# Second mixer of a three-layer kernel: gate steps shifted, compressed keys in another PSUM bank, a diagonal made earlier, scores with turned sign

## The reference, cut to what matters

```
z = rms_norm(x, ln1_g) @ w_in                       # mq mk mv mo mi mf aq akc avc aks avs akw avw ag
# mLSTM, 4 heads of 128: gates from mi, mf (log-sigmoid, running sum, running maximum), then per head
h = num / max(|den|, exp(-m));  h = rms_norm(h, mlstm_norm_g) * sigmoid(mo)
# attention, 8 heads of 64 in 2 groups, three branches, each a softmax with a distance penalty:
Kc, Vc = gelu(blocks(akc) @ ck_w1) @ ck_w2, gelu(blocks(avc) @ cv_w1) @ cv_w2      # 31 compressed keys
s = q . k / 8 - slope * distance;  p = softmax(s, masked);  o = p @ v
a = gate0 * o_compressed + gate1 * o_selected + gate2 * o_window
x = x + concat(h, a) @ w_out
```

## Time and profile before

| what | value |
|---|---|
| median of 3 runs | 1643.48 us (1639.96 to 1644.78) |
| the profiled execution's own time | 1649.33 us |
| its span, first to last instruction | 1647.6 us |
| mean granted TensorE clock | 0.985 |
| PE busy (matmul) | 1598.9 us, 97% |
| DVE busy | 1023.2 us, 62% |
| ACT busy | 706.1 us, 43% |
| POOL busy | 172.3 us, 10% |

### The profile page before, as it was taken

How to read it: one execution, slowest core, us unless ns; L and a number is a source line. 1 busy time by engine, 2 the same in 40 slices (tenths; PEclk the granted TensorE clock), 3 DMA queues, 4 the chain that set the end, 5 groups by cost and what they waited for, 6 DMA issues and landing times.

```text
span 1647.6 us, 21391 instructions
## 1 busy us (share of the span) xinstructions
PE 1598.9 (97%) x8046; PEld 1295.3 (79%) x8046; DVE 1023.2 (62%) x1926; ACT 706.1 (43%) x1391; POOL 172.3 (10%) x148
## 2 busy tenths in 40 slices
PE   7999999999998999999999999999998999999997
PEld 7888888888875788888888887766665888888887
DVE  6876666645667586766653376666666555554367
ACT  6544444333456545444432333344344344433242
POOL 0021111000012202111110000000010001110000
PEclk9999999999998999999999999999999999999998
DMA  6133333332110213333322424221110233333331
GB/s 221 52 109 96 97 101 96 103 115 97 61 58 26 75 55 100 98 94 94 101 96 98 140 98 116 53 51 39 39 39 20 90 96 96 97 97 100 96 109 64
DMA packets 91151, 143.69 MB, mean 87 GB/s; under 512 B 8740, under 2 KB 30756, under 8 KB 90920
## 3 DMA queue, kind: packets, MB, share of 16 engines
q1 hardware_dynamic: 88560, 136.58, 27.0%
q10 hardware_dynamic: 2488, 5.75, 1.1%
HBM read 140.19 MB, written 2.10 MB: 86 GB/s over the span
## 4 chain that ended last, share of the span: by engine, by line
PE 91%; DVE 4%; issue 2%; ACT 2%; DMA 1%; SPq 0%; POOL 0%; DVEq 0%; POOLq 0%; ACTq 0%
PE ps L433 23%; PE ps L435 23%; PE ps L434 23%; PE ps L1915 2%; PE ps L1917 2%; PE ps L1916 2%; PE ps L474 2%; PE ps L476 1%; PE ps L475 1%; PE ps L1597 1%; PE ps L1620 1%; PE ps L1640 1%; PE ps L1293 1%; PE ps L1322 1%; PE ps L1242 1%
## 5 line engine op out<-in xcount | busy, mean ns | idle before, releaser
L418 DVE TENSOR_TENSOR wl<-raw,wh 128x512 fp32r<-128x512 f32 (+2 forms) x425 | 307.3, 727 | 406.9 <-ACT wh L409 406.6
L409 ACT ACTIVATE wh<-raw 128x512 fp32r<-128x512 f32 (+2 forms) x425 | 264.5, 627 | 554.2 <-PE ps L435 549.6
L433 PE MATMUL ps<-Hh,wh 128*128 128x512 f32 x1148 | 453.1, 395 | 3.1 <-DVE Hl L1486 1.9
L434 PE MATMUL ps<-Hl,wh 128*128 128x512 f32 x1148 | 448.6, 391 | 0.0
L435 PE MATMUL ps<-Hh,wl 128*128 128x512 f32 x1148 | 448.5, 391 | 0.0
L433 PEld LDWEIGHTS ps<-Hh,wh 128*128 128x128 f32 x1148 | 216.3, 188 | 51.7 <-issue 2.7
L434 PEld LDWEIGHTS ps<-Hl,wh 128*128 128x128 f32 x1148 | 216.5, 189 | 45.4 <-issue 0.7
L435 PEld LDWEIGHTS ps<-Hh,wl 128*128 128x128 f32 x1148 | 216.4, 189 | 45.5
L433 PE MATMUL ps<-AH,wh 128*128 128x512 f32 x416 | 161.8, 389 | 0.0
L434 PE MATMUL ps<-AL,wh 128*128 128x512 f32 x416 | 161.8, 389 | 0.0
L435 PE MATMUL ps<-AH,wl 128*128 128x512 f32 x416 | 161.8, 389 | 0.0
(11 more groups left out here) (335 smaller groups left out, 2191.5 us busy)
## 6 DMA issues: line engine op xcount, KB each, us to landing
raw<-in_w_in SPq DMA_DIRECT2D x216, 256.0 KB, 2.7
raw<-in_w_out SPq DMA_DIRECT2D x104, 256.0 KB, 2.6
raw<-in_w_up SPq DMA_DIRECT2D x64, 256.0 KB, 2.7
raw<-in_w_down SPq DMA_DIRECT2D x32, 256.0 KB, 2.6
raw<-in_w_q SPq DMA_DIRECT2D x16, 256.0 KB, 2.6
raw<-in_w_o SPq DMA_DIRECT2D x16, 256.0 KB, 2.6
raw<-in_w_pg SPq DMA_DIRECT2D x16, 256.0 KB, 2.6
X<-in_xT SPq DMA_DIRECT2D x8, 256.0 KB, 4.6
```

The costliest lines, as they stand in the source:

```text
L409: e.activation(split_in[n][0][:, 0:width], raws[n % NRAW][:, 0:width], ACT.Copy, scale=1.0 if gain is None else gain).then_inc(s_hi, 1)
L418: e.tensor_tensor(wl[:, 0:width], raw, wh[:, 0:width].bitcast(F32), ALU.subtract).then_inc(s_lo, 1)
L433: e.matmul(b, wh[:, o:o + w], xh, start=k == 0, stop=False, skip_group_check=joined)
L434: e.matmul(b, wh[:, o:o + w], xl, start=False, stop=False, skip_group_check=joined)
```

## The change

It touches the second mixer only.

1. `gates` 1, 2, 3 and 4 stand later: after `z1` 4, `z1` 6, `z2` 0 and `z2` 2. Abs, Exp and Ln become an entry of their own on ACT, `logs`, after `z1` 3.
2. The compression uses bank `turned[7]` (`CMP_BANK`) in place of the gates' bank. `cmp` 1 no longer waits for `s_gcol` 2, but for `s_zev` 10, the end of `take 1`.
3. In beat 0, (`m`, 0, 0) stands ahead of `unit` 0, and the first two column tiles wait for `s_zev` 11 and 12 in place of 13.
4. L1892 and L1896 of step 7 (the diagonal) become an entry of their own, `lstm_diag`, ahead of `sums` in the same beat, and so ahead of that beat's split, `mtake` and `turn` on DVE; for head 3 it stands ahead of `w0` 4.
5. Queries are scaled by -0.125, the distance tables have the other sign, the maxima become minima, and the exponentials take scale -1. L1710 falls away, and with it two of DVE's own waits in a unit.

```diff
         for k in range(1, 8):
             MIX += [("z1", k)]
-            MIX += [("gates", k // 2 - (k == 2))] if k in (2, 4, 6) else [("blocks", 2 * (k // 2) + i) for i in range(2)]
-            MIX += [("gates", 1)] * (k == 3)
+            MIX += [("gates", k // 2 - 1)] if k in (2, 4, 6) else [("blocks", 2 * (k // 2) + i) for i in range(2)]
+            MIX += [("logs",)] * (k == 3)
         MIX += [("take", 1)]
         for k in range(8):
-            MIX += [("z2", k)] + [("cmp", k)] * (1 <= k <= 6) + [("gates", 4)] * (k == 0)
+            MIX += [("z2", k)] + [("cmp", k)] * (1 <= k <= 6) + [("gates", 3 + k // 2)] * (k in (0, 2))
...
         for b in range(NU + 3):
-            MIX += [("unit", b)] + [("m", b, 0)] * (b < 32) + [("sums", b)]
+            MIX += [("m", 0, 0), ("unit", 0)] if b == 0 else [("unit", b)] + [("m", b, 0)] * (b < 32)
+            MIX += [("lstm_diag", LSTM[b - 8][0])] * (b >= 8 and LSTM[b - 8][1] == 7)
+            MIX += [("sums", b)]
...
-        MIX += [("w0", 3), ("fill", 6), ("w0", 4), ("lstm", *LSTM[31]), ("w0", 5), ("w0", 6), ("fill", 7), ("w0", 7)]
+        MIX += [("w0", 3), ("fill", 6), ("lstm_diag", 3), ("w0", 4), ("lstm", *LSTM[31]), ("w0", 5), ("w0", 6), ("fill", 7), ("w0", 7)]
...
                     for g in range(2):
-                        e.tensor_tensor_reduce(Sb[u % 4][:, g, 0:L], turned[4 + g][:, 0:L], bias[:, 4 * g + r, S - L:S],
-                                               1.0, -3e38, ALU.add, ALU.max,
-                                               unit_sc(u, 0)[:, g:g + 1]).then_inc(s_vst, 1)
-                    step += 2
-                    e.wait_ge(s_vst, step)
-                    e.tensor_scalar(unit_sc(u, 1), unit_sc(u, 0), -1.0, None, ALU.mult).then_inc(s_sm, 1)
+                        m = e.tensor_tensor_reduce(Sb[u % 4][:, g, 0:L], turned[4 + g][:, 0:L],
+                                                   bias[:, 4 * g + r, S - L:S], 1.0, 3e38, ALU.add, ALU.min,
+                                                   unit_sc(u, 1)[:, g:g + 1])
+                    m.then_inc(s_sm, 1)
...
             elif s == 7:
-                c0, c1 = lane_col(h, 0), lane_col(h, 1)
-                e.wait_ge(s_mpow, h + 1)
-                e.scalar_tensor_tensor(c1, c1, 0.5, c0, ALU.mult, ALU.mult).then_inc(s_mdx, 1)
-                e.wait_ge(s_mdx, h + 1)
-                if h > 0:
-                    e.wait_ge(s_mbr, h)
-                e.tensor_tensor(DG[:, :, :], ident[:, :].unsqueeze(1).to_broadcast([P, 4, P]),
-                                c1.unsqueeze(2).to_broadcast([P, 4, P]), ALU.mult).then_inc(s_mdg, 1)
                 e.wait_ge(s_mbr, h + 1)
...
+        def dve_lstm_diag(e, h):
+            c0, c1 = lane_col(h, 0), lane_col(h, 1)
+            e.wait_ge(s_mpow, h + 1)
+            e.scalar_tensor_tensor(c1, c1, 0.5, c0, ALU.mult, ALU.mult).then_inc(s_mdx, 1)
+            e.wait_ge(s_mdx, h + 1)
+            if h > 0:
+                e.wait_ge(s_mbr, h)
+            e.tensor_tensor(DG[:, :, :], ident[:, :].unsqueeze(1).to_broadcast([P, 4, P]),
+                            c1.unsqueeze(2).to_broadcast([P, 4, P]), ALU.mult).then_inc(s_mdg, 1)
...
                     if t < 4 and t % 2 == 0 and half == 0:
-                        e.wait_ge(s_zev, 13)
+                        e.wait_ge(s_zev, 11 + t // 2)
...
-        GATE_BANK = 3
+        GATE_BANK, CMP_BANK = 3, 7
         def pe_compress(e, k):
-            hb = turned[GATE_BANK]
+            hb = turned[CMP_BANK]
             if k == 1:
                 e.wait_ge(s_w1, 32)
-                e.wait_ge(s_gcol, 2)
+                e.wait_ge(s_zev, 10)
...
+        def act_logs(e):
+            e.wait_ge(s_gst, 2)
+            e.activation(T[7][0:4, :], T[5][0:4, :], ACT.Abs).then_inc(s_gac, 1)
+            e.wait_ge(s_gac, 1)
+            e.activation(T[7][0:4, :], T[7][0:4, :], ACT.Exp, scale=-1.0).then_inc(s_gac, 1)
+            e.wait_ge(s_gac, 2)
+            e.activation(T[7][0:4, :], T[7][0:4, :], ACT.Ln, bias=1.0).then_inc(s_gac, 1)
...
-                    e.scalar_tensor_tensor(big[:, at_, :], b, 0.125, RB[:, :], ALU.mult, ALU.mult).then_inc(s_zev, 1)
+                    e.scalar_tensor_tensor(big[:, at_, :], b, -0.125, RB[:, :], ALU.mult, ALU.mult).then_inc(s_zev, 1)
```

More of the change, by code:

```diff
@@ L1650, in act_unit @@
                     pv = Sb[u % 4][:, :, 0:124]
-                    e.activation(pv, pv, ACT.Exp).then_inc(s_ex, 1)
+                    e.activation(pv, pv, ACT.Exp, scale=-1.0).then_inc(s_ex, 1)
                 else:
@@ L1655, in act_unit @@
                         sx = Sb[u % 4][:, g, 0:L]
-                        m = e.activation(sx, sx, ACT.Exp, bias=unit_sc(u, 1)[:, g:g + 1],
+                        m = e.activation(sx, sx, ACT.Exp, scale=-1.0, bias=unit_sc(u, 1)[:, g:g + 1],
                                          accum_out=unit_sc(u, 2)[:, g:g + 1])
@@ L1695, in dve_unit @@
                         e.wait_ge(s_vst, step + 1)
-                        e.tensor_reduce(cmp_sc(g, 0), pv, AX, ALU.max).then_inc(s_vst, 1)
+                        e.tensor_reduce(cmp_sc(g, 0), pv, AX, ALU.min).then_inc(s_vst, 1)
                         e.wait_ge(s_vst, step + 2)
@@ L2023, in act_gates @@
         def act_gates(e, k):
-            R = lambda i: T[i][0:4, :]
             if k == 0:
@@ L2028, in act_gates @@
                              ACT.Sigmoid).then_inc(s_gsg, 1)
[L2029 to L2034, removed]
             elif k == 4:
@@ L2091, in act_second @@
                     e.activation(hid[:, :, 0:62],
-                                 turned[GATE_BANK][:, 128:256].rearrange("p (i n) -> p i n", i=2)[:, :, 0:62],
+                                 turned[CMP_BANK][:, 128:256].rearrange("p (i n) -> p i n", i=2)[:, :, 0:62],
                                  ACT.Gelu_apprx_tanh).then_inc(s_gelu, 1)
@@ L2100, in act_second @@
                     act_gates(e, i[0])
+                elif what == "logs":
+                    act_logs(e)
                 elif what == "unit":
@@ L2176, in dve_second @@
                     dve_unit_turn(e, i[0] - 2)
+                elif what == "lstm_diag":
+                    dve_lstm_diag(e, i[0])
                 elif what == "lstm":
@@ L2487, in constants @@
     for h in range(8):
-        c[:, o + S * h:o + S * h + S] = np.where(d <= 0, d, NEG) * SLOPES[h]
+        c[:, o + S * h:o + S * h + S] = np.where(d <= 0, -d, -NEG) * SLOPES[h]
     o = CONST["swa"][0]
@@ L2498, in constants @@
             b = o + 31 * (8 * tb + h)
-            c[:, b:b + 31] = np.where(d <= 0, d, NEG) * SLOPES[h]
+            c[:, b:b + 31] = np.where(d <= 0, -d, -NEG) * SLOPES[h]
     o = CONST["sel"][0]
```

## The result

The changed kernel takes 1634.61 us, the median of 6 runs (1632.63 to 1639.78); the kernel before took 1643.57 beside it (6 runs, 1639.96 to 1646.80). The ratio is 0.9949, with an interval of 0.9934 to 0.9965: by the ratio 8.4 us less, between 5.8 and 10.8. Forecast were 1633.5, and a gain of 9.9.

What follows compares the result with a forecast made beforehand. PE's matmuls fill 97% of the span, so only PE's waits or lower clock can be won. 2.8 - 0.3 + 0.7 + 5.0 + 0.2 + 3.0 - 1.5 = 9.9 us off the median 1643.48: 1633.5, range 1629.5 to 1639.5.

Steps and rivals of the forecast that it cites:

- The gate steps: In the front (z1 and z2): with gate steps and logarithm later, `take 1` and `cmp` 1 start earlier, gain 2.8 us.
- The bank costs nothing: At the compression: the other bank removes the wait for `s_gcol` and costs nothing by itself.
- The new fall: Behind the new wait of about 3.4 us before `cmp` 1: one fall of PE's clock, minus 1.5 us.
- rival B: No new clock fall before `cmp` 1, or falls in the last beats go too: 11.5 to 14 us, 1630.5; chance 0.2.
- `gates` 4 and beat 0: Gate transposes behind `cmp` 1 cost 0.3 us; (`m`, 0, 0) ahead of unit 0 starts unit 1 0.7 us earlier.
- The diagonal: At step 7 of heads 0, 1 and 2: PE's whole wait for L1896 goes, 3 times 1.67, 5.0 us.
- Rival D, hidden anyway: PE's gains are lost to ACT's splits, `gates` 4 and DVE's unit: 1641, a gain of 2 to 3 us; chance 0.07.
- Signs: Without L1710, one or two waits for DVE in the last beats shorten by 0.1 to 0.2 each: 0.2 us.
- The two falls: The clock falls at 1185 and 1240 go with the waits before them, 1.5 us each: 3.0 us.
- A, the diagonal only: The front gives nothing and the falls at 1185 and 1240 stay: 5.0 + 0.2, up to 1 more, 1638; chance 0.2.
- C: Rival, slower: a late power holds DVE at L1892; margin about 0.8 us, 1645.6 at 4 us beyond it; chance 0.03.

Runs made afterwards that it cites:

- experiment 9: The kernel before with only the other bank (`cmp` in `turned[7]`, `cmp` 1 waiting for `s_zev` 10): 1649.41 us in one run.
- experiments 2: The changed kernel with signs and diagonal undone, so the front alone: 1644.05 us (10 runs), ratio 0.9996 to the kernel before.
- experiment 6: The changed kernel with one more power of the same size on POOL ahead of the real one: 1634.14 us in one run.
- experiment 7: The changed kernel with 96 DVE steps as small as L1710, three in each of 32 units: 1633.84 us in one run.
- experiment 10: The kernel before with only beat 0 changed, (`m`, 0, 0) ahead of unit 0: 1640.47 us in one run.
- experiment 8: The changed kernel with blocks 6 and 7 alone behind `take 1`: 1632.38 us in one run.
- experiment 1: The kernel before with the diagonal's part alone (`lstm_diag` and its list entries): 1637.82 us (10 runs), ratio 0.9965.
- experiment 3: The kernel before with the turned signs alone (minima, turned constants, no L1710): 1648.80 us in one run.
- experiments 4 and 11: The changed kernel with blocks 6 and 7 and gates 2 to 4 put later, behind `take 1`: 1630.23 us; run once more: 1631.83 us.

## Why the prediction was right

**The gate steps: 2.8 forecast, 2.82 measured.** With the 6.15 us ahead of the mark put back, L2061 ends at 1008.96 (1009.0 forecast), `take 1` starts at 1012.90 (1013.0) and `cmp` 1 at 1015.48 (1015.5). DVE's line was added up from rows and had no pause in which an error could hide. The wait was 3.07 us instead of 3.4, since PE came to it 0.3 later than laid out.

**The bank costs nothing: true only in the new list.** Alone it costs 1.15 (experiment 9), since `cmp` 1 then waits for DVE's last take. In the changed kernel that cost is inside the 3.07. What the bank allows is `gates` 4 behind `cmp` 1; in the old bank, `cmp` would have to wait for it.

**The new fall: -1.5 forecast, -1.57 measured.** It stood in each of the five profiles of kernels with this wait (the changed kernel twice, experiments 2, 6 and 7), so rival B, given 0.2, didn't come, and 1.47 of the 2.82 is lost again before unit 1. By the Trainium skill ("TensorE: Matmul & The Clock Gate", section "What's actually happening") the lower clock is the default and activity releases it; the trace agrees in so far as a fall follows this wait of 3.07 us. What the prediction drew from that rule, that one long wait is worse than two short ones, isn't shown: the two waits of before, 1.13 and 2.33 us, had one fall behind them as well (0.57 from 1010 to 1014). The front has one fall before and one after; it only stands behind the start of `cmp` 1 now.

**`gates` 4 and beat 0: -0.3 and 0.7 forecast.** Beat 0 is 0.63 (experiment 10), with the two small waits that were forecast, 0.17 and 0.27. The transposes cost nearer to 0.5: in experiment 8, without a fall, from the first `cmp` matmul to the last it takes 13.72 with them in between, 13.20 before without them, and the two parts together gave 0.10 (27.20 against 27.10).

**The diagonal: 5.0 forecast, 5.4 measured.** Of experiment 1's 8.33, the two falls are 2.88 (below); the waits themselves gave 5.4: 1.93 in each of two periods and 1.57 in the last beats (45.89 with the wait and no fall, experiment 9, against 44.32). 1.93 is more than a wait's 1.67, because idle time is counted from the modelled end of the matmul before it. Head 1 before:

```profile
1180.85 0.27 PE L1640 MATMUL ps<-ident,b_Sb 128*128 128x128 f32 x1
1182.79 1.12 PE L1800 MATMUL ps<-DG,ones 128*128 128x512 f32 x2 [1.67 <-DVE DG L1896]
1183.84 1.18 PE L1597 MATMUL ps<-b_big 64*128 64x384 f32 x4
```

From start to start it took 1.94 to L1800 and takes 0.11 now (1120.28 to 1120.39), 1.83 less; from there to the next unit it took 1.05 and takes 0.95. Together these are the 1.93. Why the second is 0.10 shorter isn't shown. Rival D, hidden anyway, fell with experiment 1.

**Signs: 0.2 forecast, 0.6 to 0.9 measured.** This term was mis-sized. The prediction looked for one or two waits in the last beats. There the turn gave 0.58 alone (experiment 3), and 0.89 with the diagonal already moved (44.32 in experiment 1 against 43.43). Five of the 32 L1710 stand in that stretch, 0.86 us by their durations. Not every step counts there in full: the 15 that experiment 7 added, 2.4 us, cost 0.6. Up to beat 31 they cost nothing, as forecast: these added steps left both periods at 51.13. Only one wait of DVE's own falls away in a unit, the one ahead of L1710, not two.

**The two falls: 3.0 forecast, 2.9 measured**: 1.55 behind head 1, and 1.33 behind head 2 (last beats of 47.22 before, 45.89 in experiment 9 without it). That the other executions might hold fewer is confirmed: over the five kernels that still had the waits of 1.67, a fall stood behind 7 of 15 of them. At 1.5 each that is 2.1 per execution, not 3.0. The prediction also said that what the profiled execution has more than the median isn't in the trace; it is: most of it lies ahead of the mark, in the 27.3 us at the lower clock. A gain of 16.7, read off the two profiles, would have been 6.15 too much.

**Rivals.** A, the diagonal only, fell in the traces, since the front's 1.35 and the two falls are there; but its sum of 5.2 to 6.2 reaches into the runs' interval of 5.8 to 10.8, so the runs alone wouldn't have told it from the forecast. For C, the margin was 0.65 us (0.8 forecast). With the power 0.33 beyond it (experiment 6), the two periods and the last beats grew by 0.6 together, about 1.9 per us (an estimate) where up to three were forecast. For B, the range's lower end is its far end and not its middle: 11.5 to 14 off the median are 1632.0 to 1629.5.

**The sum.** Front 1.35, diagonal 8.33, signs 0.60 make 10.28 of the 10.55; the rest is what the signs give more behind the diagonal. In the runs, the diagonal carries it: 5.8 of 8.4 us, the front alone nothing that can be told. The mechanism was right part by part, but the closeness of 9.9 to 8.4 is in part luck: the signs were put 0.4 to 0.7 too low and the falls of an average execution 0.9 too high, and these nearly cancel.

## What to carry to other kernels

When a late step is moved, lay out the whole line of work of the engine it sits on, and ask which piece of it the next waiter really needs: the front of this change replaced two waits by a longer one on the same engine, and 5 more us up to unit 1, 4 to the end, came from putting behind `take 1` what nobody needed yet. A step on which a matmul waits goes ahead of splits that are wanted three pieces later; here that cost nothing that could be measured, and it also took the clock's falls away. And two single profiles are compared from a fixed mark on, stage by stage, with the falls of each counted.

## What the runs showed of the hardware

- **Falls by the wait before them**, over all 14 profiled executions. Behind the 3.1 us ahead of `cmp` 1: 5 of 5. Behind the 2.33 for L2016: 5 of 5; a wait of 1.12 to 1.20 stands about 3 us ahead of it each time, so its own share isn't separated. Behind the 1.67 at the heads: 7 of 15, and behind the same three heads without the wait: none of 27. Behind the 1.36 for `take 2`: 1 of 4. Behind the 1.02 of experiment 9 and the 0.72 of experiment 8: none. With the 2.21 of the last beats: 12 of 13, in experiments 4 and 11 shortly before the wait's end. The same code with the same wait falls or doesn't from one execution to the next.
- **A fall's price depends on who sets the pace**: 1.55 to 1.59 us where PE does (head 1; `cmp`; unit 0 of experiment 9, where unit 1 comes 6.01 behind it instead of 4.42), 1.33 behind head 2, nothing measurable at the 2.21-us wait, where PE waits for ACT and DVE soon after (43.43 against 43.42, one pair), and about 1.0 for the double one of experiments 4 and 11. Why that one lasts twice as long stays open.
- **The spread from run to run goes with the clock**: the changed kernel's fastest run, 1632.63, has a mean of 0.991, and its slowest, 1639.78, one of 0.986.
- **Two powers in a row** on POOL take 1.40 and 1.01 us in experiment 6 (1.22 for the second in head 3): the first of a pair is dearer.
